# A three-part transformer layer on one core: MLA work moved ahead inside a token tile, and its first tile prepared during the last down products

## The chip, the cores and the metric

The kernel runs on one core of one Trainium2 chip. The metric is the device time of one execution in microseconds. Three runs of the kernel before gave 3411.62, 3408.42 and 3406.63 us; the median is 3408.42.

## What is computed

One layer of an encoder over 1024 prompt tokens and 512 sample tokens, width 1024, all in float32:

```python
h = modulate(rmsnorm(x, ffn1_norm), sh1, sc1)
x = x + 0.5 * g1 * swiglu(h, ffn1_wg, ffn1_wu, ffn1_wd)
h = modulate(rmsnorm(x, mix_norm), sh2, sc2)
y = token_mixing(h, ...)        # window attention heads || MLA heads, then w_out
x = x + g2 * y
h = modulate(rmsnorm(x, ffn2_norm), sh3, sc3)
x = x + 0.5 * g3 * swiglu(h, ffn2_wg, ffn2_wu, ffn2_wd)
x = rmsnorm(x, final_norm)
```

`token_mixing` starts with `z = h @ w_in` (1184 columns: 640 of window-attention q and k, 128 of its v, 256 and 128 of latents, 32 of a shared rope key). The 640 are normed per head and turned by rope. The latents are normed, then multiplied by `w_uq` and `w_ukv` to the q, k and v of eight MLA heads, which are normed and turned too. The attention itself comes after and is not touched.

## The kernel before, in words

The five engine queues are written out by hand; semaphores order them. Stages follow each other: the start, the first feed-forward block (`ffn_*(…, 0)`), the mixing preparation (`mix_*`), attention, the output projection, the second feed-forward block. Float32 products are made by splitting both factors in a high part (a rounded copy, by ACT) and a low part (the difference, by POOL or DVE) and adding three matmuls (`three_pass`, L422 to L425).

**Last round of the first feed-forward block.** PE makes 24 down products (`down_step`: 3 chunks of 512 tokens by 8 rows of the width), six matmuls each, into two PSUM banks in turn. DVE adds each to `XT` (L554). Once a chunk of `XT` is whole, the sum of its squares is wanted for the norm of the mixing stage: ACT squares eight 128x512 pieces (`sums_act`, L613), DVE adds them in four pairs (`pair_up`, L619), PE sums over partitions by four matmuls with ones (`sums_pe`, L632), ACT takes the root (`root_act`, L624) and DVE the reciprocal into `rstd_m` (`root_dve`, L638). The squares have four buffers in `x_sqm`. Between these, ACT and POOL split ten weight pieces (`mix_weight_hi` L862, `mix_weight_lo` L867; `uq`, `ukv` and eight of `win`).

**Mixing preparation.** Twelve tiles of 128 tokens go through `turns(engine, plan)`: a plan lists the stages of an engine with the lag of each in tiles, and iteration u runs stage s for tile u - lag. The stages of a tile:

- POOL `pool_x` (L1118): `hn = XT * rstd_m`; ACT `act_h`, `act_h_hi` (L941): scale, shift and high part `ht_hi`; POOL `pool_n` (L1128): low part `ht_lo`.
- PE `pe_z` in three parts (27, 27 and 18 matmuls): the projection z into three banks. ACT `act_z1` (L950) copies it to `z_sb`; `act_z2` squares the latents, then the 640 q and k columns (L961), and takes the roots (L963, L964; those of q and k, L967 and L968, after DVE's sums L1023).
- DVE `dve_z`: reciprocal (L1017), norms of the latents (L1019, L1020), sums (L1023), norm of q and k (L1030, L1032), rope (L1041 to L1046), sum (L1049).
- PE `pe_latent` (three transposes), ACT `act_l`, DVE `dve_l` (L1060): latents transposed and split; PE `pe_s` (L911), ACT `act_s`, DVE `dve_s` (L1053): the same for window q and k; SP writes them to DRAM.
- PE `pe_m`: the MLA products q and kv. ACT `act_m` copies q, its squares (L985) and v, then squares k and takes roots (L994 is the one of k). DVE `dve_m`: sum (L1066), rope (L1074 to L1079), norms (L1082, L1084), k sums (L1087, L1089), reciprocal (L1092) and k (L1098, L1099).
- PE `pe_t`: transposes of q (L901) and k (L904). ACT `act_t` and DVE `dve_t` (L1107) split them into `qT_st` and `kT_st`; SP writes them.
- POOL `pool_z`, `pool_m`: the rope tables, from rows that SP loads (`sp_rope`, `sp_ropeb`).

The order within an iteration:

```python
PE:   pe_z part 0 (u), pe_latent (u-1), pe_z part 1 (u), pe_t (u-2), pe_z part 2 (u), pe_s (u-1), pe_m (u-1)
ACT:  act_m (u-2), act_l (u-1), act_h (u+1), act_t (u-2), act_h_hi (u+1), act_s (u-1), act_z1 (u), act_z2 (u)
DVE:  dve_m (u-2), dve_l (u-1), dve_t (u-2), dve_s (u-1), dve_z (u)
POOL: pool_m (u-2), pool_x (u+1), pool_ones, pool_n (u+1), pool_z (u)
SP:   sp_rope (u), sp_ropeb (u-2), sp_m (u-2), sp_t (u-2), sp_z (u), sp_s (u-1)
```

`pe_t` waits for the end of `dve_m`, and stands in PE's queue between two parts of the next tile's projection. `pe_s` waits for L1049 of its tile and for the first L1107 of the tile before; `pe_m` for the second. `act_z1` waits for the whole projection and for L1049 of the tile before.

## Time and profile before

| | |
|---|---|
| runs, us | 3406.63, 3408.42, 3411.62 |
| profiled execution, us | 3405.11 |
| its span (first to last instruction), us | 3403.3 |
| mean granted TensorE clock | 0.968 of full speed |
| PE busy | 3180.0 us, 93% |
| DVE busy | 1466.4 us, 43% |
| ACT busy | 810.1 us, 24% |
| POOL busy | 517.8 us, 15% |

By stage, from the windows of the trace (us from the span's start): the first feed-forward block ends near 1227; the mixing preparation runs from there to 1607; attention starts near 1636. In 1300 to 1600 PE is busy 221.6 of 300 us, at granted clocks of 0.79 to 0.90; in 2500 to 3403 it is busy 894.4 of 903. A row of the timeline gives start and length of an instruction, or of a run of like ones (xN), and in brackets how long its engine had been idle and which instruction ended that. Lengths overlap where an engine is pipelined.

### The profile page before, as it was taken

How to read it: one execution, taken by the hardware profiler on the slowest of the kernel's cores; microseconds unless marked ns; L12 is line 12 of the kernel's file. 1: busy time of each engine (PE TensorE's matmuls, PEld its weight loads, DVE VectorE, ACT ScalarE, POOL GpSimd, SP SyncE). 2: the span in 40 equal slices, each digit the busy share in tenths (PEclk: the TensorE clock that was granted, in tenths of full speed). 3: DMA queues.
4: the chain of work that ended last, by engine and by line, in shares of the span. 5: the costliest groups of instructions: out<-in, count | busy, mean ns of one | idle time of the engine just before them, and what ended most of it. 6: DMA issues, size and time to landing. Idle time of an engine off the chain costs nothing.

```text
span 3403.3 us, 38874 instructions
## 1 busy us (share of the span) xinstructions
PE 3180.0 (93%) x14017; PEld 2475.8 (73%) x14017; DVE 1466.4 (43%) x2515; ACT 810.1 (24%) x1422; POOL 517.8 (15%) x303
## 2 busy tenths in 40 slices
PE   7899999999999978775799998999999999999999
PEld 2688888888888857664455555678888888888887
DVE  2566666666662246664343333154223223222224
ACT  3311111111111144553343333332111111111112
POOL 1111111111111142220000000341111111111110
PEclk9999999999999989887799999999999999999999
DMA  6112122212111112333521223221111110111112
GB/s 236 37 53 70 49 62 74 63 57 65 55 51 38 35 61 78 95 95 111 125 57 42 58 52 79 78 83 44 31 31 35 32 31 25 37 34 34 31 31 81
DMA packets 268158, 207.49 MB, mean 61 GB/s; under 512 B 16827, under 2 KB 240942, under 8 KB 268078
## 3 DMA queue, kind: packets, MB, share of 16 engines
q1 hardware_dynamic: 268078, 206.41, 20.8%
q8 instruction: 52, 0.85, 0.1%
q14 instruction: 28, 0.23, 0.0%
HBM read 169.31 MB, written 37.06 MB: 61 GB/s over the span
## 4 chain that ended last, share of the span: by engine, by line
PE 51%; DVE 5%; issue 3%; ACT 2%; SPq 1%; DMA 1%; POOL 0%; DVEq 0%; ACTq 0%; POOLq 0%
PE PS L423 12%; PE PS L424 12%; PE PS L425 12%; PE PS L1367 6%; PE PS L1318 1%; PE PS L1352 1%; PE PS L1351 1%; PE PS L1353 1%; PE PS L1331 1%; DVE z_sq L1041 1%; DVE mbuf L1484 1%; PE PS L901 1%; PE PS L1308 1%; PE PS L904 1%; PE PS L1343 0%
## 5 line engine op out<-in xcount | busy, mean ns | idle before, releaser
L423 PE MATMUL PS<-H_hi,W_hi 128*128 128x512 f32 x2304 | 906.6, 394 | 4.2 <-POOL W_lo L1667 4.2
L425 PE MATMUL PS<-H_hi,W_lo 128*128 128x512 f32 x2304 | 899.0, 390 | 0.0
L424 PE MATMUL PS<-H_lo,W_hi 128*128 128x512 f32 x2304 | 898.5, 390 | 0.0
L417 POOL TENSOR_TENSOR W_lo<-raw,W_hi 128x1024 fp32r<-128x1024 f32 x132 | 317.3, 2410 | 1839.0 <-ACT W_hi L390 1839.0
L554 DVE SCALAR_TENSOR_TENSOR XT<-PS,mod,XT 128x512 f32<-128x512 f32 x528 | 395.5, 750 | 298.4 <-PE PS L425 298.2
L423 PEld LDWEIGHTS PS<-H_hi,W_hi 128*128 128x128 f32 x2304 | 433.8, 188 | 94.0 <-issue 5.9
L425 PEld LDWEIGHTS PS<-H_hi,W_lo 128*128 128x128 f32 x2304 | 433.4, 188 | 91.8
L424 PEld LDWEIGHTS PS<-H_lo,W_hi 128*128 128x128 f32 x2304 | 433.9, 188 | 90.1 <-issue 1.4
L542 DVE TENSOR_TENSOR PS<-hid_g,PS 128x512 f32<-128x512 f32 x132 | 91.8, 696 | 832.2 <-PE PS L425 823.3
L390 ACT ACTIVATE W_hi<-raw 128x1024 fp32r<-128x1024 f32 x132 | 137.3, 1055 | 1230.7 <-PE PS L425 1230.1
L423 PE MATMUL PS<-hid_hi,W_hi 128*128 128x512 f32 x1056 | 414.6, 393 | 5.2 <-DVE XT L554 3.8
L424 PE MATMUL PS<-hid_lo,W_hi 128*128 128x512 f32 x1056 | 411.4, 390 | 0.0
L425 PE MATMUL PS<-hid_hi,W_lo 128*128 128x512 f32 x1056 | 411.3, 389 | 0.0
L408 DVE SCALAR_TENSOR_TENSOR ada_acc<-ada_r,silu_c,ada_acc 128x128 f32<-128x128 f32 x672 | 287.6, 470 | 14.8 <-DMA ada_r<-in_ada_w 1.7
L423 PEld LDWEIGHTS PS<-hid_hi,W_hi 128*128 128x128 f32 x1056 | 198.2, 188 | 56.1 <-DVE XT L554 15.4
L425 PEld LDWEIGHTS PS<-hid_hi,W_lo 128*128 128x128 f32 x1056 | 198.3, 188 | 41.4
L424 PEld LDWEIGHTS PS<-hid_lo,W_hi 128*128 128x128 f32 x1056 | 198.3, 188 | 40.1
L505 ACT ACTIVATE hid_hi<-PS 128x512 fp32r<-128x512 f32 x132 | 78.9, 598 | 590.7 <-DVE PS L542 590.7
L1438 ACT ACTIVATE probs<-PS 128x512 f32<-128x512 f32 x224 | 133.6, 596 | 255.0 <-PE PS L1353 187.7
L1484 DVE TENSOR_REDUCE mbuf<-PS 128x1 f32<-128x1024 f32 (+1 forms) x96 | 100.5, 1047 | 170.7 <-PE PS L1318 170.7
L1367 PE MATMUL PS<-probs,vv 128*66 128x512 f32 x320 | 166.1, 601 | 0.2
L1667 POOL TENSOR_TENSOR W_lo<-raw,W_hi 128x1024 fp32r<-128x1024 f32 x24 | 57.6, 2402 | 603.3 <-ACT W_hi L1663 603.1
(197 smaller groups left out, 3070.4 us busy)
## 6 DMA issues: line engine op xcount, KB each, us to landing
ada_r<-in_ada_w SPq DMA_DIRECT2D x192, 128.0 KB, 2.3
raw<-in_ffn_wg SPq DMA_DIRECT2D x44, 512.0 KB, 3.9
raw<-in_ffn_wu SPq DMA_DIRECT2D x44, 512.0 KB, 4.0
raw<-in_ffn_wd SPq DMA_DIRECT2D x44, 512.0 KB, 3.7
ada_w_sb<-in_ada_w SPq DMA_DIRECT2D x6, 2048.0 KB, 14.9
raw<-in_w_out SPq DMA_DIRECT2D x24, 512.0 KB, 4.2
scr_qb<-qT_st SPq DMA_DIRECT2D x24, 384.0 KB, 4.6
scr_kb<-kT_st SPq DMA_DIRECT2D x24, 384.0 KB, 5.8
```

Source lines behind the costliest of these rows:

```text
L390: act.activation(W_hi[:, n % WS, :], raw[:, n % RS, :], ACT.Copy).then_inc(w_hi_ready, 1)
L408: mm = dve.scalar_tensor_tensor(out=acc_, in0=w, scalar=c, in1=acc_, op0=ALU.mult, op1=ALU.add)
L417: pool.tensor_tensor(W_lo[:, n % WS, :], raw[:, n % RS, :], W_hi[:, n % WS, :].bitcast(F32), ALU.subtract).then_inc(w_ready, 1)
L423: pe.matmul(out, w_hi, m_hi, start=first, stop=False)
L424: pe.matmul(out, w_hi, m_lo, start=False, stop=False)
L425: return pe.matmul(out, w_lo, m_hi, start=False, stop=last)
L505: act.activation(hid_hi[:, t, (c - 1) * CH:c * CH], PS[:, 3 + c - 1, :], ACT.Copy).then_inc(hid_hi_done, 1)
L542: dve.tensor_tensor(PS[:, 3 + c, :], hid_g[:, t, col], PS[:, 3 + c, :], ALU.mult).then_inc(prod_done, 1)
L554: dve.scalar_tensor_tensor(out=xt, in0=PS[:, 6 + i % DS, :], scalar=hgate[:, g, m, c:c + 1], in1=xt, op0=ALU.mult, op1=ALU.add).then_inc(a ...
L1367: pe.matmul(PS[0:VW, 4, :], v, probs[:, i % PR, :], start=(t == 0), stop=(t == un.nk - 1)).then_inc(pv_done, 1)
L1438: act.activation(probs[:, i % PR, :], PS[:, 2 + i % 2, :], ACT.Exp).then_inc(exps_done, 1)
L1484: dve.tensor_reduce(m[:, piece:piece + 1], PS[:, 0:un.nk // 4, :].rearrange("p b c -> p (b c)"), AX_X, ALU.max).then_inc(reds_done, 1)
```

## The change

`mix_*` plans: the stages of DVE and ACT are cut in pieces and put in another order. For a tile u - 2 everything up to the MLA k (`dve_m`, `dve_m_norm`, `dve_k`) now comes before the window q and k of tile u - 1 (`dve_z_qk`); only the latent norms (`dve_z`, now lag 1) and one sum (`dve_z_sums`) stay ahead. ACT takes the roots of the latents before it squares the 640 columns, which moved to the next iteration. POOL makes `hn` before the tables of z and the low part after them. SP loads the second rope row one tile earlier.

The last down round: eight buffers for the squares of chunk 0 (`x_sqw`) instead of four, all of `x_sqm`'s length for chunks 1 and 2 with one more piece `x_sqa`; the ones matmuls of a chunk in two halves after down products 3 and 6 of the next chunk; those of chunk 2 around the first part of the first projection; weight copies of ACT in two runs (four pieces, then six); squares of chunks 1 and 2 wait piece by piece; `act_h(0)` and `act_h_hi(0)` move ahead of the sums of chunk 2; the reciprocal of chunk 0 in halves. `pool_n(0)` waits for the last down product.

```diff
 aZ: steps "z_copied", "c_squares", "c_root", "squares", "qk_root"
@@ ffn_pe
+                        if f == 0 and last_round(it) and c > 0 and m in (3, 6):
+                            sums_pe(pe, 1, c - 1, m // 6)
...
-                    if f == 0 and last_round(it) and c > 0:
-                        sums_pe(pe, 1, c - 1)
                 if f == 0 and last_round(it):
-                    sums_pe(pe, 1, NCH - 1)
+                    sums_pe(pe, 1, NCH - 1, 0)
@@ ffn_act
-                    for c in range(NCH):
-                        mix_weight_hi(act, ((0, 1, 2, 3), (4, 5, 6), (7, 8, 9))[c])
-                        if c > 0:
-                            root_act(act, 1, c - 1)
-                        sums_act(act, 1, c)
-                    root_act(act, 1, NCH - 1)
+                    mix_weight_hi(act, range(4))
+                    sums_act(act, 1, 0)
+                    mix_weight_hi(act, range(4, N_MW))
+                    root_act(act, 1, 0)
+                    sums_act(act, 1, 1)
+                    act.wait_ge(gate_ready, 2)
+                    act_h(act, 0)
+                    act_h_hi(act, 0)
+                    root_act(act, 1, 1)
+                    sums_act(act, 1, 2)
+                    root_act(act, 1, 2)
@@ ffn_dve
-                        if i == KD + 5:
-                            pair_up(dve, 1, 0)
-                        if i == 2 * KD + 3:
-                            root_dve(dve, 1, 0)
-                        if i == 2 * KD + 5:
-                            pair_up(dve, 1, 1)
+                        if i in (KD + 1, KD + 3):
+                            pair_up(dve, 1, 0, (i - KD) // 2)
+                        if i in (KD + 7, 2 * KD + 1):
+                            root_dve(dve, 1, 0, int(i > 2 * KD))
+                        if i in (2 * KD + 2, 2 * KD + 5):
+                            pair_up(dve, 1, 1, (i - 2 * KD) // 4)
...
+                    pair_up(dve, 1, 2)
                     root_dve(dve, 1, 1)
-                    pair_up(dve, 1, 2)
                     root_dve(dve, 1, 2)
@@ sq_slot
             if i // NCH == 1:
-                return x_sqm[:, j % 4 // 2, j % 2, 0:CH]
+                c = i % NCH
+                if c == 0 and j >= 4:
+                    return x_sqw[j % 4 // 2][:, j % 2, :]
+                if c == 2 and j == 7:
+                    return x_sqa[:, :]
+                return x_sqm[:, j % 4 // 2, j % 2, j // 4 * CH:(j // 4 + 1) * CH]
@@ sums_act
-            if b == 1:
-                act.wait_ge(acc_done, DS + (NPAIR - 1) * NCH * KD + (c + 1) * KD)
...
-                act.wait_ge(sq_used, i * NPP + j // 2 + 1)
+                if b == 1:
+                    whole = c == 0 or c == 1 and j >= 4
+                    act.wait_ge(acc_done, DS + (NPAIR - 1) * NCH * KD + c * KD + (KD if whole else j + 1))
+                    if c > 0:
+                        act.wait_ge(sq_used, (i - 1) * NPP + j // 2 + 3)
+                else:
+                    act.wait_ge(sq_used, i * NPP + j // 2 + 1)
@@ pe_z
+            if part == 0 and isinstance(u, int) and u == 0:
+                sums_pe(pe, 1, NCH - 1, 1)
@@ pool_n
+            if isinstance(u, int) and u == 0:
+                pool.wait_ge(ffn_steps, down_step(0, NPAIR - 1, NCH * KD - 1))
@@ the plans
-            turns(act, [(act_m, 2), (act_l, 1), (act_h, -1), (act_t, 2), (act_h_hi, -1), (act_s, 1), (act_z1, 0),
-                        (act_z2, 0)])
+            turns(act, [(act_m, 2), (act_z_squares, 1), (act_m_roots, 2), (act_z_roots, 1), (act_l, 1), (act_k_root, 2),
+                        (act_h, -1), (act_t, 2), (act_h_hi, -1), (act_s, 1), (act_z1, 0), (act_z2, 0)], ((act_h, 0), (act_h_hi, 0)))
-            turns(dve, [(dve_m, 2), (dve_l, 1), (dve_t, 2), (dve_s, 1), (dve_z, 0)])
+            turns(dve, [(dve_z, 1), (dve_m, 2), (dve_z_sums, 1), (dve_m_norm, 2), (dve_k, 2), (dve_z_qk, 1), (dve_l, 1),
+                        (dve_t, 2), (dve_s, 1)])
-            turns(pool, [(pool_m, 2), (pool_x, -1), (pool_ones, 0), (pool_n, -1), (pool_z, 0)])
+            turns(pool, [(pool_m, 2), (pool_x, -1), (pool_z, 1), (pool_ones, 0), (pool_n, -1)])
-            turns(sp, [(sp_rope, 0), (sp_ropeb, 2), (sp_m, 2), (sp_t, 2), (sp_z, 0), (sp_s, 1)])
+            turns(sp, [(sp_rope, 0), (sp_ropeb, 1), (sp_m, 2), (sp_t, 2), (sp_s, 1), (sp_z, 0)])
```

DVE, inside the loop over tiles, from the low part of window q and k onward, before (ISA and REGISTER_ALU rows compute semaphore targets):

```order
L1053 TENSOR_TENSOR sw_hl<-PS,sw_hl 128x640
L1016 ISA
L1017 RECIPROCAL st<-st 128x2
L1018 ISA
L1019 TENSOR_SCALAR z_sb<-z_sb,st 128x256
L1020 TENSOR_SCALAR z_sb<-z_sb,st 128x128
L1023 TENSOR_REDUCE st<-z_sq 128x10
L1029 REGISTER_ALU
L1030 RECIPROCAL st<-st 128x10
L1031 REGISTER_ALU
L1032 TENSOR_TENSOR z_sb<-z_sb,st 128x640
```

and at the same place of the changed kernel, where the loop begins right after `sw_hl`:

```order
L1240 ISA
L1047 RECIPROCAL st<-st 128x2
L1048 ISA
L1049 TENSOR_SCALAR z_sb<-z_sb,st 128x256
L1050 TENSOR_SCALAR z_sb<-z_sb,st 128x128
L1099 ISA
L1100 TENSOR_REDUCE st<-kb_sb 128x8
L1104 ISA
L1105 REGISTER_ALU
L1108 TENSOR_TENSOR kb_sb<-qb_sb,tab_bq 128x8x16 x2
```

After the norm of the latents (128x256 and 128x128) the MLA sum L1100 now follows, where before the sum and norm of the 640 columns stood. What was next to them comes only behind the MLA k:

```order
L1136 TENSOR_TENSOR kb_sb<-PS,st 128x8x64
L1137 ISA
L1137 TENSOR_TENSOR kb_sb<-krr,st 128x8x32
L1063 REGISTER_ALU
L1064 RECIPROCAL st<-st 128x10
L1065 REGISTER_ALU
L1066 TENSOR_TENSOR z_sb<-z_sb,st 128x640
L1068 ISA
L1069 REGISTER_ALU
L1075 TENSOR_TENSOR z_sq<-z_sb,tab_a 128x8x32 x2
L1075 TENSOR_TENSOR z_sq<-z_sb,tab_a 128x2x32 x2
```

L1064 to L1083 are the old L1030 to L1049: the window q and k, now after L1137 (the old L1099), which releases PE's transposes.

ACT in the last down round and up to the first copy of z, before:

```order
L862 ACTIVATE win_hi<-win_in 128x1184 x2
L613 ACTIVATE x_sqm<-XT 128x512 x8
L862 ACTIVATE win_hi<-win_in 128x1184 x3
L624 ACT_TABLE_LOAD
L624 ACTIVATE rstd_m<-PS,eps_col 128x512
L613 ACTIVATE x_sqm<-XT 128x512 x8
L862 ACTIVATE win_hi<-win_in 128x1184 x3
L624 ACTIVATE rstd_m<-PS,eps_col 128x512
L613 ACTIVATE x_sqm<-XT 128x512 x8
L624 ACTIVATE rstd_m<-PS,eps_col 128x512
L934 ACTIVATE hn<-hn,mod 128x128 x8
L941 ACTIVATE ht_hi<-hn 128x1024
```

and now:

```order
L881 ACTIVATE win_hi<-win_in 128x1184 x2
L629 ACTIVATE x_sqm<-XT 128x512 x4
L629 ACTIVATE x_sqw<-XT 128x512 x4
L881 ACTIVATE win_hi<-win_in 128x1184 x6
L640 ACT_TABLE_LOAD
L640 ACTIVATE rstd_m<-PS,eps_col 128x512
L629 ACTIVATE x_sqm<-XT 128x512 x8
L955 ACTIVATE hn<-hn,mod 128x128 x8
L962 ACTIVATE ht_hi<-hn 128x1024
L640 ACTIVATE rstd_m<-PS,eps_col 128x512
L629 ACTIVATE x_sqm<-XT 128x512 x7
L629 ACTIVATE x_sqa<-XT 128x512
```

The six weight copies stand together, all squares of chunk 0 ahead of them; `hn` and `ht_hi` of tile 0 stand before the root of chunk 1 and before the squares of chunk 2.

## Rows read from the trace of the kernel before

**Rows 1.** windows: one tile, then its transposes of qb and kb alone.
```profile
core 0: us, PE busy (x) PEld busy (x) DVE busy (x) ACT busy (x) POOL busy (x), PEclk, DMA share, GB/s
1457.19:1484.52 27.33, 21.62 (x116) 19.34 (x115) 17.08 (x31) 14.53 (x37) 7.10 (x10) 0.88 0.34 98
1502.90:1506.30 3.40, 3.38 (x17) 3.23 (x17) 0.81 (x4) 3.22 (x7) 0.00 (x0) 0.50 0.00 0
```

**Rows 2.** ACT timeline, one steady tile: start, us long, instruction, [idle before <- releaser].
```profile
1484.52 1.27 ACT L950 ACTIVATE z_sb<-PS 128x512 f32<-128x512 f32 x3
...
1486.86 0.74 ACT L961 ACTIVATE z_sq<-z_sb 128x640 f32<-128x640 f32 x1
...
1490.82 0.81 ACT L985 ACTIVATE kb_sb<-PS 128x768 f32<-128x768 f32 x1
...
1510.30 1.06 ACT L941 ACTIVATE ht_hi<-hn 128x1024 fp32r<-128x1024 f32 x1 [2.58 <-PE PS L425]
```

**Rows 3.** DVE timeline of the same tile.
```profile
1488.15 0.17 DVE L1017 RECIPROCAL st<-st 128x2 f32<-128x2 f32 x1 [2.67 <-ACT st L964]
...
1490.20 0.22 DVE L1030 RECIPROCAL st<-st 128x10 f32<-128x10 f32 x1 [0.55 <-ACT st L968]
...
1491.31 3.38 DVE L1041 TENSOR_TENSOR z_sq<-z_sb,tab_a 128x256 f32<-128x256 f32 x4
...
1496.40 0.94 DVE L1066 TENSOR_REDUCE st<-kb_sb 128x8 f32<-128x768 f32 x1
...
1502.38 0.41 DVE L1099 TENSOR_TENSOR kb_sb<-krr,st 128x256 f32<-128x256 f32 x1
...
1507.75 1.28 DVE L1107 SCALAR_TENSOR_TENSOR kT_st<-PS,par,kT_st 96x1024 fp32r<-96x1024 f32 x1 [0.31 <-ACT kT_st L1004]
```

**Rows 4.** PE timeline of the same tile.
```profile
1502.92 1.94 PE L901 MATMUL PS<-ident,qb_sb 128*96 128x128 f32 x8 [5.73 <-DVE kb_sb L1099]
...
1510.10 0.71 PE L911 MATMUL PS<-ident,z_sq 128*128 128x128 f32 x5
```

**Rows 5.** POOL timeline of the same tile.
```profile
1484.11 2.46 POOL L1128 TENSOR_TENSOR ht_lo<-hn,ht_hi 128x1024 fp32r<-128x1024 f32 x1 [16.84 <-ACT ht_hi L941]
...
1492.21 2.40 POOL L1118 TENSOR_TENSOR hn<-XT,rstd_m 128x1024 f32 x1
```

**Rows 6.** one source line over the run: DVE TENSOR_SCALAR of the ada sums, ns min/median/max.
```profile
L406 DVE TENSOR_SCALAR ada_acc<-ada_r,silu_c x96: 271/281/2432, 212.2 to 969.5; 128x128 f32<-128x128 f32 x96
```

**Rows 7.** ACT copies of the projection, first, second and last of 12 tiles.
```profile
1272.80 0.58 ACT L950 ACTIVATE z_sb<-PS 128x512 f32<-128x512 f32 x1
...
1292.05 1.27 ACT L950 ACTIVATE z_sb<-PS 128x512 f32<-128x512 f32 x3
...
1563.31 1.28 ACT L950 ACTIVATE z_sb<-PS 128x512 f32<-128x512 f32 x3
```

**Rows 8.** last down round and first projection: ACT, then POOL.
```profile
1199.20 2.19 ACT L613 ACTIVATE x_sqm<-XT 128x512 f32<-128x512 f32 x4 [2.40 <-DVE XT L554]
...
1212.24 3.34 ACT L862 ACTIVATE win_hi<-win_in 128x1184 fp32r<-128x1184 f32 x3
...
1231.66 8.00 POOL L867 TENSOR_TENSOR win_lo<-win_in,win_hi 128x1184 fp32r<-128x1184 f32 x3 [9.99 <-ACT win_hi L862]
```

**Rows 9.** the same stretch: DVE, then PE.
```profile
1224.92 1.28 DVE L619 TENSOR_TENSOR x_sqm<-x_sqm 128x512 f32<-128x512 f32 x2
...
1237.61 5.34 DVE L619 TENSOR_TENSOR x_sqm<-x_sqm 128x512 f32<-128x512 f32 x2
...
1227.25 1.88 PE L632 MATMUL PS<-x_sqm,ones 128*128 128x512 f32 x4
...
1256.04 0.77 PE L423 MATMUL PS<-win_hi,ht_hi 128*128 128x512 f32 x1 [7.40 <-issue]
```

**Rows 10.** DVE timeline behind the last copy of z.
```profile
1583.83 1.28 DVE L1107 SCALAR_TENSOR_TENSOR kT_st<-PS,par,kT_st 96x1024 fp32r<-96x1024 f32 x1 [0.43 <-ACT kT_st L1004]
...
1595.69 0.49 DVE L1074 TENSOR_TENSOR kb_sb<-qb_sb,tab_bq 128x128 f32<-128x128 f32 x2 [4.30 <-POOL tab_bq L1157]
```

More of the change, by code:

```diff
@@ L965, in act_z2, with act_z_squares, act_z_roots @@
                .then_inc(*aZ.tick("c_root"))
+        def act_z_squares(act, u):
+            act.wait_ge(aZ.sem, aZ.at(u, "c_squares"))
+            act.activation(z_sq[:, 0:640], z_sb[:, 0:640], ACT.Square).then_inc(*aZ.tick("squares"))
+        def act_z_roots(act, u):
             act.wait_ge(vZ.sem, vZ.at(u, "sums"))
@@ L1189, in sp_t, with turns @@
                     sp.dma_start(scr[i, :, :, tok(u)], st_[:, i, :, :].bitcast(F32)).then_inc(written, 16)
-        def turns(eng, plan):
+        def turns(eng, plan, done=()):
             lags = [lag for _, lag in plan]
@@ L1197, in turns @@
                 for stage, lag in plan:
-                    if 0 <= u - lag < NT:
+                    if 0 <= u - lag < NT and (stage, u - lag) not in done:
                         stage(eng, u - lag)
```

21 lines of the change are left out of this document (16 added, 5 removed).

## The prediction, made before the changed kernel was run

> **What bounds the kernel now.** I read the whole page first, then windows, then the timelines of each engine. In both feed-forward blocks PE is busy throughout, and the change touches neither of them except the last down round of the first. In the mixing preparation a tile takes 27.33 us, of which PE is busy 21.62, DVE 17.08, ACT 14.53 and POOL 7.10, at a mean granted clock of 0.88 [rows 1]. So no engine bounds it; a ring over several does. With t0 the moment ACT begins to copy z (1484.52), DVE starts on that tile at t0 + 3.63, after the squares of the 640 columns [rows 2, 3]; works on z until 1496.40, that is 8.25 us; on the MLA part of the tile before from 1496.40 to 1502.79, 6.39 us; and only then PE may transpose qb and kb, having stood idle for 5.73 us [rows 4]. Behind these transposes stand the last part of the projection, the transposes of window q and k (1510.10), ACT's `ht_hi` (1510.30) and the next copy of z (27.33 after t0). Two things make the ring longer than its work: the rope of z took 3.38 us for four small instructions, up to the end of POOL's `hn` (1492.21 + 2.40 = 1494.61) [rows 3, 5]; and after the idle time PE ran its transposes at a granted clock of 0.50, the 1.2 GHz level, in 3.40 us [rows 1].
>
> Ahead of the tiles lies a second gap: the last down product ends at 1227.25, the first projection starts at 1256.04, 28.8 us later [rows 9]. In between ACT waits for PE to free its four square buffers, the last weight splits run on POOL until 1239.66 [rows 8], and two pair additions on DVE take 5.34 us instead of 1.28 [rows 9].
>
> **Steady tiles: the new ring, again from t0.** The squares of the 640 columns (0.74 and a hand-over of 0.03) go behind the roots of the latents: DVE could start at 3.63 - 0.77 = 2.86. But POOL ends the low part of h at t0 + 2.05, turns a small table (I take 0.35) and starts `hn` at 2.4, until 4.8 [rows 5]. The norms of the latents are TENSOR_SCALAR; no row of before has one of them beside such a POOL instruction. The nearest row is the TENSOR_SCALAR of the ada sums: median 281 ns, largest 2432, the length of one POOL instruction [rows 6]. I take the same here: DVE starts at 4.8. Lower bound 2.9 (no blocking), though q is squared by ACT only at about 4.4, so that at most 0.9 can be won; upper bound one more POOL instruction later, 7.2.
>
> - Latent norms: z's head took 1488.15 to 1489.65 (1490.20 less the 0.55 idle) [rows 3], two thirds of a microsecond of it the norms: 5.4.
> - MLA sum, rope, norms, k: 6.39, with the sum of the 640 columns (0.8) now in the middle: 12.6. Before, it was 18.3. ACT's pieces fit between: it squares and takes roots for both tiles in time.
> - PE comes from the two first parts of the next projection. They take about 9.9 from a start near 3.5, so the transposes start at 13.4, not at 12.6: the wait of 5.73 is gone and PE arrives last. Warm, they take 1.7 instead of 3.4; the last projection part ends at 18.4.
> - DVE meanwhile does window q and k: 1490.20 to 1496.40 is 6.20, less the 2.3 spent blocked, 3.9 to 4.1: 16.7. Then the low part of the latents 0.8 and that of qT 1.3 (the one of kT in [rows 3]): 18.8. PE's window transposes wait for that, a little after PE is free (18.4); 0.6 for them, 0.6 for ACT's copy, 0.3 of hand-overs: next copy of z at **20.3**.
>
> PE's own work per tile is 21.62 - 1.7 = 19.9 with warm transposes [rows 1], so PE and DVE's ring are nearly level; 20.3 stands. POOL's `hn` now ends before the rope of z begins, and the tables follow it at once (5.9), far ahead of their use. SP's second rope row comes a tile early. Of twelve copies the second is at 1292.05 and the last at 1563.31, ten periods of 27.13 [rows 7]: 271.3 becomes 203, a gain of **68.3**. Bounds: 19.5 per tile (PE alone, without hand-overs) gives 76; 22.5 gives 46.
>
> **The end of the stage.** Behind the last copy the MLA products of the last tile wait for DVE's low part of kT of the tile before: in the ring 19.1 after the copy (no `hn` any more), before at 1583.83 + 1.28 - 1563.31 = 21.8 [rows 7, 10], so 2.7. Then DVE waited 4.30 us for the rope table, whose row SP had issued behind the writes [rows 10]; now it is loaded a tile earlier. Together **7.0**, between 2.7 and 9. What follows (writes landing, loads of attention) is untouched and starts earlier as a whole.
>
> **The start.** Eight squares of chunk 0 take 8 x 0.55 from 1199.20, to 1203.6, then six weight copies of 1.11 to 1210.3 [rows 8]. So POOL's six splits of 2.67 run without gaps from 1204.8 [rows 8], where before they ran in threes with ten idle microseconds between. DVE's pair additions now fall among them. The pair at 1237.61 shows the price: it began, finished only after the split's end at 1239.66, and the second waited for `hn` [rows 8, 9]. I let every pair addition wait for the POOL instruction under way, and POOL and DVE take turns:
>
> - chunk 1: pairs 1 and 2 end at 1204.8, pairs 3 and 4 at 1211.5; since PE has two banks, it stands about 3.5 us; the four ones matmuls (about 0.94 each, four rows to two of them [rows 9]) lie inside. Its products end at 1217.0.
> - chunk 2: the reciprocal comes in two halves and is no longer than before; POOL's splits end at 1222.3, `hn` of tile 0 runs to 1225.0, the pairs of chunk 1 wait for it and PE stands 2.7. The last product ends at 1235.2: **8 later** than before.
> - `hn`, its scaling and `ht_hi` of tile 0 are done by 1229.3. The low part waits for the last product, 1235.3 to 1237.7; two pairs of chunk 2 are caught by it and by `hn` of tile 1. PE has the half sum at 1242.4 and starts the projection then, 13.6 earlier than 1256.04. The other two ones matmuls go inside it (+1.9): the first copy of z at 1260.8 against 1272.80 [rows 7], a gain of **12.0**. Bounds: without any blocking the products end at 1231 and the gain is 19; with one POOL instruction more before each pair it is 6. The second copy follows the first by 19.25 as before.
>
> **Sum.** 12.0 + 68.3 + 7.0 = 87.3. The profiled execution took 3405.11 (span 3403.3); it becomes 3317.8. The median of the runs lies 3.3 above it: 3408.4 - 87.3 = **3321**.
>
> **Rivals.**
>
> *The clock stays low at the transposes.* Everything above assumes that PE's short waits (0.4 for window q and k, 0.5 for kT) don't bring it down to 1.2 GHz. Against it: the 0.50 of [rows 1] came after 5.73 us idle. For it: two or three waits per tile remain. Then the transposes cost 3.4 again and what follows starts slower: 2.2 per tile, 22.5, gain 12 + 46 + 7 = 65: 3343. The Trainium skill (TensorE: Matmul & The Clock Gate, "A second HAM failure mode: psum-queue depth-cycling") describes a PE that idles briefly between groups of matmuls and swings between its two clocks though each wait is short. By that section this rival would be the likely case; the trace speaks for the other, as PE works for some 18 us between the waits.
>
> *The wait moves instead of going.* If both the latent norms and the MLA rope are caught by POOL, or ACT, which now serves two tiles alternately with DVE, answers late at each of its four hand-overs, the ring gets 3 to 4 us longer: 24 per tile, gain 12 + 31 + 7 = 50: 3358. For it: all seven hand-overs of a tile now stand in one chain. Against: ACT is busy 14.53 of 27.33 [rows 1].
>
> *Slower.* Window q and k are now last on DVE, and PE's window transposes, ACT's copy of z, and through PE's fixed order the next projection stand behind them. If DVE is caught by POOL at every instruction with two inputs in SBUF, as the pair at 1237.61 was [rows 9], not only at the latent norms, the ring grows: three more POOL instructions of 2.4 to 2.7 per tile (tables, low part, `hn`), and the 0.8 to 1 of each ACT answer behind them, are 8. The point is 7.0 more on DVE per tile; at 8, 28.3 per tile, ten tiles lose 12; the pair additions of the down round, caught twice each, put the first projection at 1264, 8 late; the end gives 7 back: 3408 + 12 + 8 - 7 = 3421. Against it: POOL is busy 7.1 us per tile [rows 1], and its low part falls where DVE is nearly idle.
>
> **How the numbers follow.** Forecast (3305 to 3333) 0.66; clock low (3335 to 3350) 0.16; wait moved (3350 to 3390) 0.14; no change or slower 0.04. The likeliest is 3321. The range must hold eight in ten: from 3304 (19.5 per tile and a little more at the start) to 3346, which takes in most of the clock rival. A measurement of this kernel can tell 0.2%, 7 us, from no change: faster 0.96, same 0.02, slower 0.02.
>
> **What the profile would show.** Right: copies of z 20 to 21 apart; no idle time of 5 us before the transposes of qb, and a granted clock near 1.00 over the tile; L1049's successor for the latents idle until the end of `hn`; last down product near 1235 and the first projection near 1242; no wait for the rope table in the last tile. Wrong: the transposes at 1.9 us each, which is the clock rival; DVE idle while ACT works on small roots, which is the moved wait; pair additions of 3 us in great number, with PE idle in the down round for over 10 us, which is the way to slower.

## The result, and the profile after

Four runs of the changed kernel took 3315.0 to 3319.2 us, median **3316.43**; four of the kernel before beside them 3405.82 to 3411.62, median 3407.53. The ratio is 0.9732, 95% interval [0.9715, 0.9749]: 2.7% faster. The forecast was 3321, its range 3304 to 3346. The profiled execution took 3316.62 us, its span 3314.8 (before 3405.11 and 3403.3).

From the page of the changed kernel, span, busy time of PE, and the granted clock in 40 slices of 83 us:

```profile
span 3314.8 us, 38929 instructions
...
PE 3157.2 (95%) x14017; PEld 2456.4 (74%) x14017; DVE 1465.3 (44%) x2516; ACT 809.9 (24%) x1422; POOL 518.1 (16%) x303
...
PEclk9899999999999999996989999999999999999999
```

Before, the mean granted clock of the execution was 0.968; now it is 0.979. The one dark slice in the middle (6) is the end of the stage and the wait for attention's loads.

**Steady tiles.** Windows of two neighbouring tiles of the changed kernel, each from copy of z to copy of z:

```profile
core 0: us, PE busy (x) PEld busy (x) DVE busy (x) ACT busy (x) POOL busy (x), PEclk, DMA share, GB/s
1342.24:1362.29 20.05, 19.91 (x119) 18.18 (x118) 15.89 (x31) 14.65 (x37) 6.62 (x10) 1.00 0.48 141
1362.29:1382.20 19.91, 18.93 (x113) 16.80 (x112) 16.36 (x31) 14.54 (x36) 7.53 (x10) 1.00 0.44 129
```

Beside [rows 1] the tile is 7.3 us shorter; ACT has as much to do as before, DVE and POOL nearly so, and the clock is 1.00 in place of 0.88. PE is busy 19.42 us on average of the two tiles (the cut at the copy of z gives the first some matmuls of the second), 2.2 less than the 21.62 before, and idle for 0.56: it has become the bound. The copies of z, ACT timeline of the changed kernel, first, second, one tile and last:

```profile
1263.25 1.26 ACT L971 ACTIVATE z_sb<-PS 128x512 f32<-128x512 f32 x3
...
1282.35 1.27 ACT L971 ACTIVATE z_sb<-PS 128x512 f32<-128x512 f32 x3
...
1362.29 1.27 ACT L971 ACTIVATE z_sb<-PS 128x512 f32<-128x512 f32 x3
...
1382.20 1.28 ACT L971 ACTIVATE z_sb<-PS 128x512 f32<-128x512 f32 x3
...
1481.80 1.28 ACT L971 ACTIVATE z_sb<-PS 128x512 f32<-128x512 f32 x3
```

The ten periods from the second copy to the last take 199.45 us, 19.95 each; before 271.26 [rows 7]: **71.8** less. The same tile on DVE (t0 = 1362.29), then on POOL, then on PE:

```profile
1365.15 0.17 DVE L1047 RECIPROCAL st<-st 128x2 f32<-128x2 f32 x1 [1.90 <-ACT st L983]
1365.35 1.77 DVE L1049 TENSOR_SCALAR z_sb<-z_sb,st 128x256 f32<-128x256 f32 x1
1367.04 0.76 DVE L1050 TENSOR_SCALAR z_sb<-z_sb,st 128x128 f32<-128x128 f32 x1
1367.72 0.94 DVE L1100 TENSOR_REDUCE st<-kb_sb 128x8 f32<-128x768 f32 x1
...
1374.43 0.42 DVE L1137 TENSOR_TENSOR kb_sb<-krr,st 128x256 f32<-128x256 f32 x1
...
1377.86 0.83 DVE L1083 TENSOR_TENSOR z_sq<-z_sb,z_sq 128x640 f32<-128x640 f32 x1
```

```profile
1364.55 2.42 POOL L1156 TENSOR_TENSOR hn<-XT,rstd_m 128x1024 f32 x1
1366.91 0.81 POOL L1175 TENSOR_TENSOR tab_a<-gw_a,rope_in 128x256 f32<-128x256 f32 x1
```

```profile
1374.99 1.06 PE L922 MATMUL PS<-ident,qb_sb 128*96 128x128 f32 x8
...
1380.71 0.77 PE L932 MATMUL PS<-ident,z_sq 128*128 128x128 f32 x5 [0.55 <-DVE qT_st L1145]
1381.90 0.44 PE L425 MATMUL PS<-uq_hi,cT_hi 128*128 128x384 f32 x1 [0.42 <-DVE kT_st L1145]
```

DVE starts at t0 + 2.86, as early as the new place of the squares allows. Its first norm of the latents (L1049) takes 1.77 us, where the same instruction before (L1019) took 0.35, and ends just behind POOL's `hn` (1364.55 + 2.42 = 1366.97); in the tiles beside this one it takes 1.30. The second (L1050) takes 0.76 instead of 0.30 and ends with the table that POOL makes next. The MLA k is ready at t0 + 12.56, window q and k at 16.40. The transposes of qb and kb (L922, L925) follow PE's projection with no idle time and take 1.06 us for eight instead of 1.94 [rows 4]: they run at the upper clock level, 2.4 GHz. What PE still waits is 0.55 and 0.42 us, in every second tile.

**The end.** After the last copy of z the last `kT_st` (L1145) starts at 1516.32, 34.5 us later; before 42.3 (1605.58 less 1563.31). The last tile's rope (the old L1074, [rows 10]) no longer waits for its table:

```profile
1506.80 0.49 DVE L1108 TENSOR_TENSOR kb_sb<-qb_sb,tab_bq 128x128 f32<-128x128 f32 x2
...
1516.32 1.28 DVE L1145 SCALAR_TENSOR_TENSOR kT_st<-PS,par,kT_st 96x1024 fp32r<-96x1024 f32 x1
```

**The start.** DVE in the last down round of the changed kernel, then PE, then POOL:

```profile
1208.53 5.33 DVE L635 TENSOR_TENSOR x_sqw<-x_sqw 128x512 f32<-128x512 f32 x2
...
1226.56 3.16 DVE L635 TENSOR_TENSOR x_sqm<-x_sqm 128x512 f32<-128x512 f32 x2
...
1238.90 0.75 DVE L561 SCALAR_TENSOR_TENSOR XT<-PS,mod,XT 128x512 f32<-128x512 f32 x1 [2.26 <-PE PS L427]
1239.57 5.69 DVE L635 TENSOR_TENSOR x_sqm<-x_sqm 128x512 f32<-128x512 f32 x3
```

```profile
1214.58 0.79 PE L425 MATMUL PS<-hid_hi,W_hi 128*128 128x512 f32 x1 [3.02 <-DVE XT L561]
...
1245.81 1.42 PE L425 MATMUL PS<-win_hi,ht_hi 128*128 128x512 f32 x1
```

```profile
1207.43 17.05 POOL L886 TENSOR_TENSOR win_lo<-win_in,win_hi 128x1184 fp32r<-128x1184 f32 x6 [1.30 <-ACT win_hi L881]
```

All of this stage stands 2.80 us later in this execution than in the one of before (first squares 1202.00 against 1199.20 [rows 8]). Of this 2.12 are there at the second reciprocal of the start (56.11 against 53.99), in a part in which no code differs; where the other 0.68 come from was not looked into. Counted from the first squares: end of the last down product on PE 36.9 (before 28.2), first projection 43.8 (before 56.8), first copy of z 61.25 (before 73.60): **12.35** less.

**The account**, by the two spans, in us: ahead of the first squares +2.8; start -12.35; first period -0.15; ten periods -71.8; end -7.75; attention and what is behind it +0.75. Sum -88.5, the difference of the spans.

### The profile page after: what moved, and what is told of

The parts are those of the page before. It is cut to its first block, busy times and chain, and to the rows that moved or that the text cites. A ratio compares the mean times of both kernels' runs of the same rounds, so it can differ in the third digit from the quotient of the medians.

```text
span 3314.8 us, 38929 instructions
## 1 busy us (share of the span) xinstructions
PE 3157.2 (95%) x14017; PEld 2456.4 (74%) x14017; DVE 1465.3 (44%) x2516; ACT 809.9 (24%) x1422; POOL 518.1 (16%) x303
## 4 chain that ended last, share of the span: by engine, by line
PE 53%; DVE 4%; issue 2%; ACT 1%; SPq 1%; DMA 0%; DVEq 0%; POOL 0%; ACTq 0%
PE PS L425 13%; PE PS L427 13%; PE PS L426 13%; PE PS L1408 6%; PE PS L1359 1%; PE PS L1393 1%; PE PS L1392 1%; PE PS L1394 1%; PE PS L1372 1%; DVE mbuf L1525 1%; PE PS L1349 1%; PE PS L1384 0%; PE PS L1385 0%; PE PS L1415 0%; PE PS L1353 0%
```

## The experiments

All ratios and times come from 4 or 5 runs each beside the kernel before on the same chip (its medians there: 3407.53, 3408.43, 3407.42 and 3409.14 us). "Start" is from the first squares of chunk 0 to the first copy of z, "period" the mean of the ten from the second copy to the last, "end" from the last copy to the start of the last `kT_st`.

| kernel | time, us | ratio, 95% interval | start | period | end |
|---|---|---|---|---|---|
| before | 3407.42 to 3409.14 | 1 | 73.60 | 27.13 | 42.27 |
| changed | 3316.43 | 0.9732 [0.9715, 0.9749] | 61.25 | 19.95 | 34.52 |
| new round, old order | 3386.87 | 0.9931 [0.9914, 0.9947] | 64.34 | 25.95 | 40.93 |
| old round, new order | 3331.97 | 0.9772 [0.9756, 0.9788] | 74.44 | 19.94 | 34.39 |
| before, rope row early | 3390.00 | 0.9944 [0.9928, 0.9961] | 73.75 | 25.95 | 37.67 |
| before, 44 idle matmuls | 3429.95 | 1.0057 [1.0040, 1.0074] | 73.71 | 29.02 | 42.58 |
| before, 22 idle matmuls | 3381.49 | 0.9924 [0.9908, 0.9941] | 73.77 | 24.45 | 40.74 |
| changed, 22 idle matmuls | 3359.34 | 0.9861 [0.9844, 0.9877] | 60.04 | 24.12 | 33.51 |
| changed, an eighth of `hn` | 3313.68 | 0.9725 [0.9709, 0.9741] | 64.35 | 19.38 | 34.63 |
| before, row early, root first | 3388.92 | 0.9950 [0.9933, 0.9966] | 74.41 | 25.73 | 37.67 |
| changed once more | 3317.39 | 0.9736 [0.9723, 0.9749] | 59.96 | 19.93 | 34.79 |
| changed, pairs on POOL | 3317.67 | 0.9734 [0.9720, 0.9747] | 61.36 | 19.94 | 34.25 |
| changed, `hn` later | 3318.10 | 0.9736 [0.9723, 0.9749] | 64.14 | 20.15 | 34.84 |
| changed, both of these | 3319.68 | 0.9729 [0.9715, 0.9744] | 61.27 | 20.15 | 34.92 |

### 1. The new round alone

The changed kernel with the order of stages of before, the rope row's lag included:

```diff
-            turns(act, [(act_m, 2), (act_z_squares, 1), (act_m_roots, 2), (act_z_roots, 1), (act_l, 1), (act_k_root, 2),
-                        (act_h, -1), (act_t, 2), (act_h_hi, -1), (act_s, 1), (act_z1, 0), (act_z2, 0)], ((act_h, 0), (act_h_hi, 0)))
+            turns(act, [(act_m, 2), (act_m_roots, 2), (act_k_root, 2), (act_l, 1), (act_h, -1), (act_t, 2), (act_h_hi, -1),
+                        (act_s, 1), (act_z1, 0), (act_z2, 0), (act_z_squares, 0), (act_z_roots, 0)], ((act_h, 0), (act_h_hi, 0)))
-            turns(dve, [(dve_z, 1), (dve_m, 2), (dve_z_sums, 1), (dve_m_norm, 2), (dve_k, 2), (dve_z_qk, 1), (dve_l, 1),
-                        (dve_t, 2), (dve_s, 1)])
+            turns(dve, [(dve_m, 2), (dve_m_norm, 2), (dve_k, 2), (dve_l, 1), (dve_t, 2), (dve_s, 1), (dve_z, 0),
+                        (dve_z_sums, 0), (dve_z_qk, 0)])
-            turns(pool, [(pool_m, 2), (pool_x, -1), (pool_z, 1), (pool_ones, 0), (pool_n, -1)])
+            turns(pool, [(pool_m, 2), (pool_x, -1), (pool_ones, 0), (pool_n, -1), (pool_z, 0)])
-            turns(sp, [(sp_rope, 0), (sp_ropeb, 1), (sp_m, 2), (sp_t, 2), (sp_s, 1), (sp_z, 0)])
+            turns(sp, [(sp_rope, 0), (sp_ropeb, 2), (sp_m, 2), (sp_t, 2), (sp_z, 0), (sp_s, 1)])
```

> The changed kernel with its new last down round, but the order of the tiles as before on ACT, DVE, POOL and SP. My theory (three separate gains: about 12.3 us at the start, 7.2 per tile in ten tiles, 7.7 at the end) expects a tile of 27.3 us again, the first copy of z about 12 us earlier than before, and 3395 us in all. Rival A, the new round is only worth something together with the new order (the early first tile is eaten by the waits of the old ring): 3405 or more. Rival B, the start is worth more than the trace shows since the granted clock stays up: 3388 or less.

Measured 3386.87: 21.6 us less than before, more than the theory gave to the start. The number lies in rival B's range, but not for its reason. The trace says why: the start is 9.3 us shorter, but the period is 25.95 instead of 27.13 too. The edit was not clean. Where `act_z2` is cut in pieces, the root of the latents' norm stands ahead of the 640 squares, as in the changed kernel. DVE's first norm then starts 0.8 us earlier and POOL's `hn` meets other instructions. From DVE's timeline here:

```profile
1444.36 0.17 DVE L1047 RECIPROCAL st<-st 128x2 f32<-128x2 f32 x1 [1.90 <-ACT st L983]
...
1447.50 1.03 DVE L1075 TENSOR_TENSOR z_sq<-z_sb,tab_a 128x256 f32<-128x256 f32 x4
...
1449.21 2.48 DVE L1080 TENSOR_TENSOR z_sb<-z_sb,tab_a 128x128 f32<-128x128 f32 x1
```

In this tile (copy of z at 1441.50) the four rope instructions run at 1.03 where [rows 3] show 3.38, and `hn` holds L1080 instead; that exchange alone is worth little here (DVE's chain up to the MLA k takes 14.50 us, before 14.63), so that most of the gain is the earlier start. So of the 21.6 some 11.8 belong to the ring of the tile, which the new order shortens anyway, and 9.3 and 1.3 to start and end.

### 2. The new order alone

The changed kernel with the last down round of before (four square buffers, ones matmuls by whole chunks, weights in three runs), all plans new:

```diff
-                        if f == 0 and last_round(it) and c > 0 and m in (3, 6):
-                            sums_pe(pe, 1, c - 1, m // 6)
+                    if f == 0 and last_round(it) and c > 0:
+                        sums_pe(pe, 1, c - 1)
...
+            if b == 1:
+                act.wait_ge(acc_done, DS + (NPAIR - 1) * NCH * KD + (c + 1) * KD)
```

> The last down round as before, with the new order of the tiles. My theory: a tile of 20.0 us, the first copy of z at about 1272.8 as before, no wait for the rope row at the end, 3407.5 - 72 - 7.7 = 3328 us. Rival A, the two halves of the change depend on each other: 3345 or more, tiles longer than 21 us.

Measured 3331.97, 76.5 us less than before. Start as before (74.44), period 19.94 and end 34.39 as in the changed kernel: ten periods give 71.9, the end 7.9. So five sixths of the whole gain are the order of the stages, and the round is worth what the changed kernel gains beyond, about 15 us. The two halves add to 98.0, 6.9 more than the 91.1 of the whole: the 11.8 us that experiment 1 gained in its tiles lie in both, and its profiled start was one of the longer ones (64.34 against 61.25, see experiment 7). My expectation for this run was 3328.

### 3. The second rope row alone

```diff
-            turns(sp, [(sp_rope, 0), (sp_ropeb, 2), (sp_m, 2), (sp_t, 2), (sp_z, 0), (sp_s, 1)])
+            turns(sp, [(sp_rope, 0), (sp_ropeb, 1), (sp_m, 2), (sp_t, 2), (sp_z, 0), (sp_s, 1)])
```

> The kernel before with one number changed: SP loads the second rope row one tile earlier (lag 1 instead of 2). My theory: the tiles stay at 27.3 us, since POOL's 3 us wait for this row is off the ring, and the last tile loses its 4.3 us wait: 3403 us. Rival, POOL's hn starts 3 us earlier and no longer blocks the rope of z on DVE (3.38 us for four instructions, 1.1 unblocked): up to 2.2 us per tile, 3381 us. Rival, the load was never late for anything that counts: 3407.5.

Measured 3390.00, 18.4 us less, by one figure in SP's plan. The end is 4.6 shorter, as the row of [rows 10] said. The rest is in the tiles, which get 1.2 us shorter each: POOL's `tab_bq` no longer waits for its row, so `hn` behind it starts earlier and holds another piece of DVE's chain. POOL, then DVE, in a tile of this kernel:

```profile
1480.87 2.40 POOL L1118 TENSOR_TENSOR hn<-XT,rstd_m 128x1024 f32 x1
```

```profile
1481.99 1.97 DVE L1032 TENSOR_TENSOR z_sb<-z_sb,st 128x640 f32<-128x640 f32 x1
1483.99 1.04 DVE L1041 TENSOR_TENSOR z_sq<-z_sb,tab_a 128x256 f32<-128x256 f32 x4
```

L1032 takes 1.97 instead of 0.82 (1.15 lost), the four of L1041 1.04 instead of 3.38 (2.34 won): 1.19 us, and nearly as much in every tile. (The periods still vary, from 25.3 to 26.8 us; what varies is PE's stretch from the transposes of qb to those of the window, 6.4 to 7.8 us, where before it took 7.2 to 7.8.) My own expectation had missed it; the rival had it, at up to 2.2 us per tile. In the changed kernel both effects are inside the 71.8 and the 7.75. Whether the changed order would work with the old lag was not tried: there SP's second row of tile u - 2 would stand behind the first row of tile u, which waits for tables that POOL makes only after the second.

### 4. The price of the clock

Before's order, with idle matmuls of ones on ones ahead of the transposes, in the time in which PE has nothing to do. Nothing of the computation changes. First with 44 of them:

```diff
         def pe_t(pe, u):
+            pe.wait_ge(aM.sem, aM.at(u, "q_copied"))
+            for i in range(44):
+                pe.matmul(PS[:, 6, 0:P], ones[:, :], ones[:, :], start=True, stop=True)
             pe.wait_ge(vM.sem, vM.at(u, "k_rope"))
```

> The kernel before with 44 extra 128x128 matmuls of ones by ones on PE ahead of the transposes of qb and kb, where it stood idle for 5.7 us: they fill about 5 us of that and feed nothing. They price the clock alone. My theory: the transposes run at 2.4 GHz instead of 1.2 (1.75 us instead of 3.45) and the products behind them start at full clock, so a tile shortens by 2 to 2.4 us, to about 25.1, and the whole by 20 to 24 us: 3385. That would make the clock 2.2 of the 7.2 us per tile, the order 5.0. Rival, the low clock there costs nothing as the ring is bound elsewhere: 3407; or the filling delays the transposes: 3415 or more.

Mis-sized: each of these float32 matmuls appears as two records, and 88 records fill 9.98 us, not 5. From PE's timeline, the filling and the transposes:

```profile
1509.70 9.98 PE L900 MATMUL PS<-ones 128*128 128x128 f32 x88
1519.52 1.04 PE L904 MATMUL PS<-ident,qb_sb 128*96 128x128 f32 x8
```

The k heads were ready at 1514.28 (L1102 at 1513.87, 0.41 long), the transposes came 5.2 us later, and still the tile is only 1.9 us longer than before. With 22:

> The kernel before, with 22 idle matmuls of ones (44 records, by the run with twice as many 0.113 us each, so 5.0 us) put into the 5.73 us in which PE waits ahead of the transposes of the heads. Theory (the clock is paid at the transposes and at the projections behind them, and the ring of the tile goes through both): the transposes run at 1.04 us for eight in place of 1.94, and a tile takes 27.33 - 3.4 = 23.9 us, 3.4 being what the run with 44 showed once its 5.1 us of delay are taken off; the time is 3408 - 11 x 3.4 - 0.5 = 3370. Rival (the clock saves no more than the transposes' own 1.6 us): tile 25.7, time 3390. Second rival (the clock is worth nothing, as another wait ends last): 3408.

```profile
1453.68 5.07 PE L900 MATMUL PS<-ones 128*128 128x128 f32 x44
1458.93 1.07 PE L904 MATMUL PS<-ident,qb_sb 128*96 128x128 f32 x8 [0.18 <-DVE kb_sb L1102]
```

Measured 3381.49, 25.9 us less than before, period 24.45: between the theory (3370) and the first rival (3390). No work was taken away and no engine's order changed; matmuls were *added*, and a tile lost 2.7 us. The transposes still start 0.14 us after the k heads, as before, so the filling delays nothing.

Not all of it is clock. In the first nine of the ten tiles the mean fell from 27.46 to 24.52, by 2.9 us. From the first transpose of qb to the first of the window (L911 before) PE takes 7.18 to 7.80 us in these tiles before, 7.33 on average, and 5.02 to 5.05 here: **2.3 us** are the clock, as the transposes take 1.04 to 1.07 instead of 1.94, and the projection behind them runs at full speed at once. The rest is on DVE. Its chain from the reciprocal of the latents (L1017 before) to the MLA k (L1099) takes 14.62 us before and 13.97 on average here, since `hn` starts 10.1 us after the copy of z instead of 7.7 (the table ahead of it waits 5.45 us for its rope row, before 2.98) and meets other instructions. DVE in the tile of the rows above:

```profile
1447.93 1.03 DVE L1044 TENSOR_TENSOR z_sq<-z_sb,tab_a 128x256 f32<-128x256 f32 x4
...
1451.72 2.24 DVE L1077 TENSOR_TENSOR kb_sb<-qb_sb,tab_bq 128x128 f32<-128x128 f32 x2
```

The four rope instructions of z take 1.03 instead of 3.38 [rows 3], the two of L1077 (the old L1074) 2.24 instead of 0.49. With 44 matmuls the same chain took 13.45 from the second tile on, and PE's stretch 4.98: of the 3.4 us that I had read there as the clock, 1.2 were this. So of the 7.2 us that the change takes from a tile some 2.2 to 2.3 are the clock, which is also by how much PE's busy time fell (21.62 to 19.42), and the rest is order.

### 5. Is PE the bound now?

The same 22 matmuls at the same place in the changed kernel:

> The changed kernel with the same 22 idle matmuls at the same place in PE's program. Theory (PE is the bound now, a tile is PE's 19.5 us and at most 0.5 of waiting): a tile takes 20.0 + 4.5 to 5.0 = 24.5 to 25.0 us, the time is 3316.4 + 12 x 4.8 = 3374, the DVE idle grows by as much. Rival (the ring through DVE still sets the tile, PE's busy time holds slack that the records do not show): the filling costs less than 2 us per tile, time under 3340.

```profile
1375.00:1399.15 24.15, 24.15 (x159) 22.45 (x159) 16.44 (x31) 14.52 (x37) 7.09 (x9) 1.00 0.38 111
```

Measured 3359.34, 42.9 more than the changed kernel, where I had expected 58; the period is 24.12, 0.4 to 0.9 less than I had expected. It grows by 4.17 of the 5.07 us put in, and PE has no idle time left at all. What made the old kernel faster costs the new one four fifths of its length. PE is the bound, with 0.9 us per tile of slack, of which the trace of the changed kernel shows some 0.5 as idle time. The rival of a hidden ring through DVE is out.

From the other side, POOL's product `hn` computed for one eighth of its elements from tile 2 on (seven eighths are left out):

```diff
-            pool.tensor_tensor(hn[:, :, :], XT[:, :, tok(u)], rstd_m[:, None, tok(u)].to_broadcast([P, KD, P]), ALU.mult) \
-                .then_inc(*gN.tick("x"))
+            if static and u < 2:
+                pool.tensor_tensor(hn[:, :, :], XT[:, :, tok(u)], rstd_m[:, None, tok(u)].to_broadcast([P, KD, P]), ALU.mult) \
+                    .then_inc(*gN.tick("x"))
+            else:
+                pool.tensor_tensor(hn[:, 0:1, :], XT[:, 0:1, tok(u)], rstd_m[:, None, tok(u)], ALU.mult) \
+                    .then_inc(*gN.tick("x"))
```

> The changed kernel with POOL's product hn computed for only one eighth of its elements from tile 2 on (seven eighths of hn are left out), so that POOL no longer holds up DVE's first normalisation. Theory (PE is the bound): DVE's L1049 falls from 1.77 to 0.35 us and its chain is 1.9 us shorter, but the tile only loses the waits that PE still has, 20.0 to 19.5 us; time 3316.4 - 5 = 3311. Rival (the DVE chain is the bound of the new tile): 1.9 us less per tile, 3316.4 - 20 = 3296.

```profile
1345.78 0.53 DVE L1049 TENSOR_SCALAR z_sb<-z_sb,st 128x256 f32<-128x256 f32 x1
```

```profile
1342.71:1362.29 19.58, 19.58 (x118) 17.89 (x117) 14.79 (x31) 14.58 (x36) 5.06 (x10) 1.00 0.49 140
```

L1049 takes 0.53, L1137 ends 1.1 us sooner after the copy, and the tile gains 0.57 (19.38): ten periods 5.7. The medians differ by 2.8; the profiled execution had one of the longer starts (64.35, see experiment 7), those of the others are not known. The theory holds: of 1.1 us on DVE about as much reaches the tile as PE still waited.

### 6. The old order at its best

Experiments 1 and 3 had each shortened the old ring by 1.2 us per tile. Both together, on the kernel before (POOL's wait for the last down product ahead of its first low part is kept too):

```diff
-            act.activation(z_sq[:, 0:640], z_sb[:, 0:640], ACT.Square).then_inc(*aZ.tick("squares"))
...
+        def act_z_squares(act, u):
+            act.wait_ge(aZ.sem, aZ.at(u, "c_squares"))
+            act.activation(z_sq[:, 0:640], z_sb[:, 0:640], ACT.Square).then_inc(*aZ.tick("squares"))
...
-            turns(act, [(act_m, 2), (act_l, 1), (act_h, -1), (act_t, 2), (act_h_hi, -1), (act_s, 1), (act_z1, 0),
-                        (act_z2, 0)])
+            turns(act, [(act_m, 2), (act_m_roots, 2), (act_k_root, 2), (act_l, 1), (act_h, -1), (act_t, 2), (act_h_hi, -1),
+                        (act_s, 1), (act_z1, 0), (act_z2, 0), (act_z_squares, 0), (act_z_roots, 0)])
...
-            turns(sp, [(sp_rope, 0), (sp_ropeb, 2), (sp_m, 2), (sp_t, 2), (sp_z, 0), (sp_s, 1)])
+            turns(sp, [(sp_rope, 0), (sp_ropeb, 1), (sp_m, 2), (sp_t, 2), (sp_z, 0), (sp_s, 1)])
```

> The kernel before, in its old order of stages, with two small edits: the second rope row is requested one tile earlier, and the root of the latent's norm stands ahead of the 640 squares on ACT. The row alone gave a period of 25.9 (1.1 less than before), the root (with the new last round) 26.2. Theory (the two shorten different pieces of the ring and add up): period 25.0, the eleven periods 25 us shorter, the end 4.6 shorter, time 3408.4 - 29 = 3379. Rival (both act through the same overlap of hn with DVE's instructions, so the second adds nothing): 3390.

Measured 3388.92, period 25.73, 0.2 less than with the row alone. Even that is not in the steady tiles: the first nine of the ten periods are 26.00 on average against 26.03, and the tenth, of the last tile, beside which POOL has no `hn` to make, is 23.32 against 25.27. DVE starts 0.77 us earlier, but `hn` starts 4.8 us after the copy of z in both, and the norm of the 640 columns waits for it: 2.77 us here, 1.97 with the row alone, its end 7.9 us after the copy in both. The rival was right.

### 7. Three attempts to beat the changed kernel

Four kernels on one chip, the changed one among them.

> The changed kernel once more, as the base for the three beside it: 3316, 0.9732 of before. Its start (squares of the first chunk to the first copy of z) was 61.25 us in the profiled execution, but the same code took 60.0 and 64.3 in two of the experiments: the theory is that PE's wait of 3 us in the middle of the last down round is followed by a low granted clock in some executions and not in others, so 60 to 64.5 is expected, and nothing between.

Measured 3317.39, start 59.96. PE in the middle of the same round, in this execution and in the one with an eighth of `hn` (nothing differs in this stage):

```profile
1213.95 0.50 PE L425 MATMUL PS<-hid_hi,W_hi 128*128 128x512 f32 x1 [2.95 <-DVE XT L561]
...
1215.45 1.88 PE L648 MATMUL PS<-x_sqw,ones 128*128 128x512 f32 x4
```

```profile
1213.81 0.80 PE L425 MATMUL PS<-hid_hi,W_hi 128*128 128x512 f32 x1 [3.02 <-DVE XT L561]
...
1216.53 3.58 PE L648 MATMUL PS<-x_sqw,ones 128*128 128x512 f32 x4
```

The wait for DVE's pair additions is 2.95 and 3.02; behind it the four ones matmuls take 1.88 in the one and 3.58 in the other, that is, they ran at the upper clock level or at the lower. The window from 1210 to 1220 has a granted clock of 1.00 in the first and 0.66 in the second (0.66 also with `hn` later, start 64.14; 0.83 in the first profile of the changed kernel, whose start of 61.25 lies between, against my "nothing between"). Behind PE's next wait of 2.4 us the four ones matmuls again take 1.96 in the first and 3.62 in the second. This is where starts of 60.0 and of 64.3 us of the same code come from.

> The changed kernel with three edits at its start: POOL adds the pairs of chunk 0 behind its fourth weight piece (DVE added them so far), POOL's hn of tile 1 waits for the last pairs, and the ones matmuls of the last chunk's first half stand behind the first part of the first projection. Theory (what is left of the start is DVE's locked pair additions that hold up the down products, and PE's wait for the pairs of the last chunk): PE no longer waits 3.0 and 2.4 us in the round nor 3.2 us behind it, the first copy of z comes 4 to 6 us earlier, 56 us after the squares, time 5 less than the changed kernel's in this batch. Rival (POOL's 16 x 512 columns of weights in two runs are the bound: 4.9 us of pairs put its hn(0) and ht_lo(0) as much later): no gain, or 2 slower.

```diff
-                        if f == 0 and last_round(it) and c > 0 and m in (3, 6):
+                        if f == 0 and last_round(it) and c > 0 and m in (5 - c, 6):
...
-                if f == 0 and last_round(it):
-                    sums_pe(pe, 1, NCH - 1, 0)
...
-                        if i in (KD + 1, KD + 3):
-                            pair_up(dve, 1, 0, (i - KD) // 2)
...
+                if i == 4:
+                    pair_up(pool, 1, 0)
...
-                sums_pe(pe, 1, NCH - 1, 1)
+                sums_pe(pe, 1, NCH - 1)
...
+            if static and u == 1:
+                pool.wait_ge(sq_paired, 2 * NCH * NPP)
```

Measured 3317.67, no difference (changed once more: 3317.39). The wait went elsewhere. POOL, DVE and PE:

```profile
1209.58 16.13 POOL L884 TENSOR_TENSOR win_lo<-win_in,win_hi 128x1184 fp32r<-128x1184 f32 x6
```

```profile
1220.03 9.13 DVE L631 TENSOR_TENSOR x_sqm<-x_sqm 128x512 f32<-128x512 f32 x2
```

```profile
1228.70 3.74 PE L644 MATMUL PS<-x_sqm,ones 128*128 128x512 f32 x4 [8.41 <-DVE x_sqm L631]
```

POOL's six splits now run until 1225.7 and `hn` until 1228.0; DVE came to the pairs of chunk 1 sooner, at 1220.03, and two additions took 9.13 us between them. PE's first stall was gone, but then it stood 8.41 us instead of 3.0 and 2.4. Moving work to POOL had lengthened the stretch in which POOL holds DVE up.

> The changed kernel with POOL's product hn behind the rope tables and the key's rotation instead of ahead of them, one place later in POOL's plan. Theory (as PE is the bound, only the waits of PE can be had: 0.56 us per tile when seven eighths of hn were left out): DVE's L1049 takes 0.35 instead of 1.77 us, hn holds up L1108 to L1113 instead, a tile gets 0 to 0.5 us shorter, time 0 to 5 less. Rival (the rotation's instructions are held as long as the norm was): no difference.

```diff
-            turns(pool, [(pool_m, 2), (pool_x, -1), (pool_z, 1), (pool_ones, 0), (pool_n, -1)])
+            turns(pool, [(pool_m, 2), (pool_z, 1), (pool_x, -1), (pool_ones, 0), (pool_n, -1)])
```

```profile
1348.61 0.35 DVE L1049 TENSOR_SCALAR z_sb<-z_sb,st 128x256 f32<-128x256 f32 x1
...
1349.88 0.95 DVE L1100 TENSOR_REDUCE st<-kb_sb 128x8 f32<-128x768 f32 x1 [0.72 <-ACT kb_sb L1010]
1350.95 1.73 DVE L1108 TENSOR_TENSOR kb_sb<-qb_sb,tab_bq 128x128 f32<-128x128 f32 x2
```

```profile
1349.93 2.40 POOL L1156 TENSOR_TENSOR hn<-XT,rstd_m 128x1024 f32 x1
```

Measured 3318.10, no difference in time; by the trace a tile is 0.2 us longer. L1049 is free (0.35), and L1108 is held instead (1.73 for two that took 0.49). Of the 1.4 us won at one place 1.2 are lost at the next, and before L1100 DVE now waits 0.72 for ACT.

> The two before it together: the gains add up, 5 to 9 us less than the changed kernel in this batch, about 3309. Rival (hn of tile 1 behind POOL's rope tables comes into the first tiles' path): no more than either alone.

Measured 3319.68, not the 3309 of the theory; from 3310.12 to 3322.01, the widest spread of all: two of five were near 3310, neither of them profiled, so what they did differently stays open. By medians nothing beats the changed kernel.

## Why the prediction was right

- **Steady tile, 20.3, measured 19.95.** The term that carries four fifths of the gain was read from [rows 2 to 5] moment by moment, and the moments hold. DVE free of `hn` at t0 + 4.8: 1366.97 is 4.68. Norms done at 5.4: 5.51. MLA k at 12.6: 12.56. Window q and k at 16.7: 16.40. Only PE was put too late: it begins the next projection at 2.7, not 3.5, so its transposes start at 12.7, not 13.4, and it is ready for the window transposes before DVE, as forecast, but waits 0.55 and only every second tile. Ten periods give 71.8, not 68.3; this is the largest miss, 3.5 us, and its sign is that of the 0.35 per tile.
- **Latent norms held by POOL.** A guess from [rows 6], since no row of before had the pair. It was right to 0.1 us. Experiment 5 (an eighth of `hn`) showed it to be nearly free, as PE arrives last anyway. I had written that at most 0.9 could be won there: 1.1 were on DVE's chain, and 0.57 on the tile.
- **Clock.** I had costed its return at 2.2 us per tile by the rows at either level; experiment 4 puts it at 2.2 to 2.3. The rival by which it stays low did not come: the granted clock of a tile is 1.00. It had counted two or three waits per tile; there are two, of 0.55 and 0.42 us, and only in every second tile. A rule of the Trainium skill (TensorE: Matmul & The Clock Gate, "A second HAM failure mode: psum-queue depth-cycling") would have had it swing. In the steady tiles the trace does not agree. In the down round something like it exists: after one wait of 3.0 us the level fell in some executions and not in others.
- **The start, 12.0, measured 12.35** in the profiled execution; last down product 8 later foreseen, 8.7 measured; first projection 13.6 earlier foreseen, 13.0 measured; PE's two stalls 3.5 and 2.7 foreseen, 3.02 and 2.44 measured. By its own terms the sum gives 11.7 (13.6 less 1.9), not 12.0. That the first copy gains nearly as much as the projection is the clock, for which the sum had no term: PE's products go at the lower level for the first 5.4 us of the projection before, and for 2.5 us now. Nor had it one for the clock after the first stall, which spreads the gain from 9.3 to 13.6; that the profiled execution lies so near to 12.0 is luck to that extent.
- **The end, 7.0, measured 7.75**: both parts there: the low part of `kT` ends 18.5 us after the last copy instead of 21.8 (19.1 foreseen), and the rope row's 4.3 (4.6 by experiment 3).
- **Wait moved, slower.** Neither came. ACT's hand-overs to DVE stayed as they were (0.24 to 0.37), and of a tile's three larger POOL instructions `hn` held DVE up by 1.4 us at most and the table behind it by 0.5 (L1050, 0.76 for 0.30), while the one DVE instruction beside the low part of h (L1087, one input in PSUM) took its usual 0.82.
- **What I had not seen.** The second rope row was costed for the end only. Experiment 3 shows it alone worth 11.8 us in the old tiles, since it sets when `hn` starts. In the changed order POOL's `hn` was timed rightly, so the sum did not suffer; as a statement on the row it was wrong, and so was my expectation of 3403 for it.
